# Fourteen products of constants on the TensorE between the router's products and the rank counts of a mixture-of-experts layer

## Chip, cores and metric

The kernel runs on one core of a Trainium2 chip, in one launch. The metric is device time in microseconds (us), the median over executions; the kernel before has 1560.44 us (median of 3 executions, 1560.36 to 1561.08).

## What is computed

One decoder layer in float32 on 256 tokens of width 2048, with 16 learned tokens in front. A combined input projection feeds three kinds of heads (HGRN2, mLSTM, Mamba-2), an output projection and a residual follow, then the part that matters here, a mixture of 32 experts with its router. Cut from the reference:

```
t = rmsnorm(h)                                    # 256 tokens x 2048 (and 16 that are dropped)
g_sel    = argmax(t @ w_group + b_group)          # one of 4 groups
e_logits = t @ w_router[g_sel] + b_router         # 8 experts in the group
top_v, top_i = top_k(e_logits, 2)                 # two experts for a token
rank of a token inside its expert = how many tokens before it chose the same expert
for every expert e, on the rows of its tokens:
    hidden = silu(xb @ w1[e]) * (xb @ w3[e]);  y = hidden @ w2[e]
out[token] += y * weight
```

## The kernel before

The program is written by hand, one instruction stream for each engine, ordered by semaphores; nothing is scheduled by a planner, so each queue runs in the order of the source.

**Up to the router.** The TensorE makes 52 input tiles of 272 columns (`tile`, `product`, line 1231) with the heads' products between them, then 16 output tiles of 256 columns (`mixed`, line 1274). After each output tile `by_rows` turns it into rows by two transposes (line 1471) and adds its part of the router's logits (line 1476, 36 columns). After the last `by_rows` the TensorE waits for semaphore `pairs`.

**Routing.** Meanwhile ScalarE sums squares (line 732) and VectorE runs `routing` (lines 292 to 332): logits, best group, two best experts, and `chosen`, a table of ones and zeros, tokens by experts. Line 332 signals `pairs`. The TensorE then counts ranks: five products with 32 columns each through `product` (line 1231 again, into bank 7), and signals `ranks`. VectorE makes the rank table (lines 335, 337) and the choice of rows for the first expert (line 1118).

**Experts.** An expert holds up to 32 token rows. For each one the TensorE does, in this order: `up` (line 1528: w1 in its first half, w3 in its second), `tokens` for the next expert (line 1511), `turn_hidden` (line 1536), `turn_tokens` (line 1518), `combine` of the expert before (line 1563: 8 products that use 32 of the 128 rows, each followed by an addition on VectorE, line 1145), `spread` (line 1543) and `down` (line 1552: w2). For expert 0 `tokens(0)` and `turn_tokens(0)` stand ahead of `up(0)`, with a copy by ScalarE after each (lines 744 and 748).

**Weights.** Each expert has three matrices of 4 MB (w1, w3, w2), so 96 transfers, all issued by SyncE's queue into four slots of SBUF. The first two are issued during the output projection (lines 416 and 418), the third and fourth after the last output tile and the last router product (lines 420 and 423). Every later one (lines 429, 433, 436) waits until the product that read its slot is done; the fifth waits for the first half of `up(0)`:

```
            sp.dma_start(eslot(3), matrix(1, 0)).then_inc(m_in[3], 16)
            used = (s["h1_ps"], s["h3_ps"], s["y_ps"])
            for m in range(4, 16):
                sp.wait_ge(used[(m - 4) % 3], (m - 4) // 3 + 1)
                sp.dma_start(eslot(m % 4), matrix(m // 3, m % 3)).then_inc(m_in[m % 4], 16)
```

**The end.** After the last transfer the TensorE still has the second half of `up(31)`, a `combine`, `down(31)` and a `combine`; ScalarE and VectorE then normalise and the result is stored. PSUM bank 1, `pb[1]`, is used by `spread` alone, first for expert 0. `ones` is a constant tile of 128 rows and 272 columns, filled at the start; T is 272, P 128.

Of the kernel before, what the change touches and what calls it, by code (L numbers as in the profile page):

```python
# [28 lines left out]
def hymba_moe_layer(nc, x, meta_tokens, hg_lb_logits, norm_mix_w, w_in, hg_norm_w, ml_b_i, ml_b_f,  # L29
# [11 lines left out]
    P = 128  # L41
# [3 lines left out]
    T = NM + SEQ  # L45
# [38 lines left out]
    FROM = [NM if t in range(Z0, Z0 + 8) or t in range(HQ, HQ + 4) or t in range(HG_, HG_ + 4)  # L84
            or t in range(MQ, MQ + 2) or t in range(MO, MO + 4) else 0 for t in range(NP_)]
    AT = {t0: sum(m for _, m in ORDER[:i]) for i, (t0, n) in enumerate(ORDER)}
    NIN, NOUT = NP_, KD

# [9 lines left out]
    with ctx:  # L98
        def sb(name, shape, dt=f32):
            return ctx.enter_context(nc.sbuf_tensor(name, shape, dt))  # L100
# [57 lines left out]
        ones = sb("ones", [P, T])  # L158
# [30 lines left out]
        pb = [ctx.enter_context(nc.psum_tensor(f"bank{i}", [P, 512], f32)) for i in range(8)]  # L189
# [350 lines left out]
        def _(act):  # L540
# [21 lines left out]
            for a, (_, n) in enumerate(TT):  # L562
                act.wait_ge(X_IN[a][0], 16 * X_IN[a][1])
                if a:
                    act.wait_ge(s["act_steps"], step.n)
                step.link(V.activation(junk[0:n, :], xin[0:n, a, :], ACT.Square, accum_out=ss3[0:n, a:a + 1]))
# [234 lines left out]
        def _(dve):  # L801
# [17 lines left out]
            for a, (_, n) in enumerate(TT):  # L819
                last = V.tensor_scalar(dg[0:n, a, 0:n], ident[0:n, 0:n], rs3[0:n, a:a + 1], None, ALU.mult)  # L820
# [403 lines left out]
        def _(pe):  # L1224
            V = nc.tensor
# [240 lines left out]
            def by_rows(k):  # L1466
                pe.wait_ge(s["in_ev"], 4 + NIN + k + 1)
                if k % 4 == 0 and k:
                    pe.wait_ge(s["t_ev"], NA * (k // 4))
                for a in range(NA):  # L1470
                    last = V.transpose(pb[5 + a][:, (k % 4) * P:(k % 4 + 1) * P],
                                       hT[:, k, NM + a * P:NM + (a + 1) * P], ident[:, :])
                    if k % 4 == 3:
                        last.then_inc(s["t_ps"], 1)
                for a in range(NA):
                    last = V.matmul(pb[(4, 7)[a]][:, 0:LG], hT[:, k, NM + a * P:NM + (a + 1) * P], wr[:, k, :],
                                    start=k == 0, stop=k == KD - 1)
                if k == KD - 1:
                    last.then_inc(s["lg_ready"], 1)
# [17 lines left out]
                by_rows(u - NIN - 1)  # L1497
            by_rows(NOUT - 1)

            pe.wait_ge(s["pairs"], 1)  # L1500
            for a in range(NA):
                product(pb[7][:, a * NE:(a + 1) * NE],
# [135 lines left out]
```

## Time and profile before

| | |
|---|---|
| median of 3 executions | 1560.44 us (1560.36 to 1561.08) |
| the profiled execution: its own time | 1565.83 us |
| the profiled execution: span of its instructions | 1564.1 us |
| TensorE busy | 1437.0 us (92%) |
| VectorE, ScalarE, GpSimd busy | 445.7, 310.0, 43.6 us |
| mean granted TensorE clock | 0.868 of full |
| read from HBM | 482.21 MB, 310 GB/s over the span |
| expert weights | 96 transfers of 4096 KB |

All durations of the trace are from the one profiled execution, whose time lies 5.39 us above the median. A granted clock of 1.00 is 2.4 GHz and one of 0.50 is 1.2 GHz; a number between them is a mean over a stretch. A float32 product stands in the trace as two matmul records, a transpose as one, so the five rank counts are ten records.

### The profile page before, as it was taken

The numbers are of one execution on the slowest core, as the hardware profiler recorded it, in microseconds if no ns is written. First come the engines' busy times: TensorE is split into PE (matmuls) and PEld (weight loads), VectorE is DVE, ScalarE is ACT, GpSimd is POOL, SyncE is SP. The second block draws the span as 40 slices with busy tenths as digits, with TensorE's granted clock in tenths as the row PEclk, the third lists the DMA queues.
The fourth block names the chain that finished last, engine by engine and source line by source line (L and its number), as shares of the span: only waits on it lengthen the run. The fifth ranks groups of instructions, "written<-read, shape, count | busy, mean of one in ns | idle before, by whom it ended". The sixth has DMA issues, their size and how long they took to land.

```text
span 1564.1 us, 18289 instructions
## 1 busy us (share of the span) xinstructions
PE 1437.0 (92%) x7667; PEld 786.7 (50%) x7667; DVE 445.7 (28%) x1033; ACT 310.0 (20%) x462; POOL 43.6 (3%) x77
## 2 busy tenths in 40 slices
PE   6999999999999997989988999889989998988986
PEld 3888888878888885323323323323323323323331
DVE  4312543341222002443312312212212313222213
ACT  2111423112123011212111112112112112112112
POOL 2000000000000011000000000000000000000002
PEclk9999999999999997888787688788788788788786
DMA  6444343445346645899999999999999999999992
GB/s 172 144 137 132 106 118 108 127 142 158 108 151 252 228 149 215 362 436 430 431 430 429 433 432 432 431 431 432 432 432 431 431 432 433 432 431 431 432 430 100
DMA packets 103512, 485.05 MB, mean 310 GB/s; under 512 B 19580, under 2 KB 89368, under 8 KB 90648
## 3 DMA queue, kind: packets, MB, share of 16 engines
q1 hardware_dynamic: 101424, 478.78, 75.9%
q0 software_dynamic: 1024, 3.37, 0.7%
q10 hardware_dynamic: 1016, 2.19, 0.4%
q8 instruction: 38, 0.62, 0.2%
q14 instruction: 10, 0.08, 0.0%
HBM read 482.21 MB, written 2.12 MB: 310 GB/s over the span
## 4 chain that ended last, share of the span: by engine, by line
PE 66%; DMA 30%; DVE 2%; ACT 1%; issue 0%; SPq 0%; ACTq 0%; DVEq 0%
DMA big<-in_moe_w_dram 30%; PE bank L1231 25%; PE bank L1563 9%; PE bank L1528 8%; PE bank L1274 7%; PE bank L1552 6%; PE bank L1511 2%; PE bank L1536 2%; DVE big L1145 2%; PE bank L1308 1%; PE bank L1287 1%; PE bank L1242 1%; PE bank L1259 1%; PE bank L1543 1%; DMA big<-in_x_dram 1%; PE bank L1352 1%
## 5 line engine op out<-in xcount | busy, mean ns | idle before, releaser
L1231 PE MATMUL bank<-big 128*128 128x272 f32 (+1 forms) x1664 | 380.1, 388 | 0.0
L1231 PEld LDWEIGHTS bank<-big 128*128 128x128 f32 x1664 | 313.6, 190 | 54.8 <-issue 0.4
L1563 PE MATMUL bank<-big 32*128 32x512 f32 x512 | 281.2, 935 | 32.8 <-DVE big L1145 31.8
L1528 PE MATMUL bank<-big 128*32 128x512 f32 x2048 | 239.7, 611 | 56.5 <-DMA big<-in_moe_w_dram 55.8
L1145 DVE TENSOR_TENSOR big<-big,bank 128x512 f32<-128x512 f32 x256 | 168.5, 685 | 165.1 <-PE bank L1563 163.9
L1563 PEld LDWEIGHTS bank<-big 32*128 32x128 f32 x512 | 94.6, 251 | 175.0 <-DVE big L1145 164.4
L1552 PE MATMUL bank<-big 128*32 128x512 f32 x1024 | 179.8, 866 | 0.1
L1528 PEld LDWEIGHTS bank<-big 128*32 128x32 f32 x2048 | 62.2, 112 | 228.0 <-issue 144.8
L1132 DVE COPY big<-bank 128x512 f32<-128x512 f32 x32 | 22.1, 692 | 415.0 <-PE bank L1528 415.0
L761 ACT ACTIVATE big<-bank 128x512 f32<-128x512 f32 x32 | 19.1, 597 | 481.6 <-PE bank L1552 481.6
L1274 PE MATMUL bank<-big 128*128 128x256 f32 x512 | 113.9, 381 | 0.0
L1274 PEld LDWEIGHTS bank<-big 128*128 128x128 f32 x512 | 96.3, 190 | 12.6
L1552 PEld LDWEIGHTS bank<-big 128*32 128x32 f32 x1024 | 39.8, 152 | 121.5 <-issue 121.2
L593 ACT ACTIVATE big<-bank 128x272 f32<-128x272 f32 (+1 forms) x52 | 20.4, 392 | 297.1 <-PE bank L1231 297.1
L1536 PEld LDWEIGHTS bank<-selq,big 128*128 128x128 f32 x512 | 59.6, 191 | 26.8 <-issue 26.8
L1511 PE MATMUL bank<-big 128*32 128x512 f32 x512 | 62.5, 607 | 1.2 <-DVE big L1118 1.2
L1536 PE MATMUL bank<-selq,big 128*128 128x32 f32 x512 | 63.1, 277 | 0.0
L744 ACT ACTIVATE big<-bank 128x512 f32<-128x512 f32 x32 | 19.1, 597 | 214.9 <-PE bank L1511 214.9
L752 ACT ACT_TABLE_LOAD x31 | 39.8, 1283 | 0.6
L757 ACT ACT_TABLE_LOAD x31 | 39.8, 1283 | 0.6
L1113 DVE TENSOR_TENSOR big<-big,bank 128x256 f32<-128x256 f32 x16 | 6.7, 421 | 110.9 <-PE bank L1274 110.9
L1511 PEld LDWEIGHTS bank<-big 128*32 128x32 f32 x512 | 16.6, 111 | 39.8 <-issue 39.8
(261 smaller groups left out, 762.0 us busy)
## 6 DMA issues: line engine op xcount, KB each, us to landing
big<-in_moe_w_dram SPq DMA_DIRECT2D x96, 4096.0 KB, 30.4
big<-in_w_in_dram SPq DMA_DIRECT2D x26, 2048.0 KB, 8.3
big<-in_w_out_dram SPq DMA_DIRECT2D x8, 2048.0 KB, 8.4
big<-gate_rows POOLq DMA_DIRECT2D x8, 272.0 KB, 3.8
out_dram<-big SPq DMA_DIRECT2D x4, 512.0 KB, 3.9
big<-gate_rows POOLq DMA_DIRECT2D x2, 544.0 KB, 5.8
big<-in_x_dram SPq DMA_DIRECT2D x1, 1024.0 KB, 8.3
big<-in_norm_ffn_w_dram ACTq DMA_DIRECT2D x1, 1024.0 KB, 4.3
```

What stands on the lines that cost most here:

```text
L593: V.activation(proj[:, TILES[u], FROM[TILES[u]]:T], pb[u % 4][:, FROM[TILES[u]]:T], func).then_inc(s["in_ev"], 1)
L752: V.activation(hs1.rearrange("t (k p) -> t k p", p=P), pb[2][:, :].rearrange("t (p k) -> t k p", k=KF), ACT.Copy).then_inc(s["h1_ev"], 1)
L757: V.activation(ssb, pb[4][:, 0:KF * CAP], ACT.Silu).then_inc(s["silu_ev"], 1)
L1132: V.tensor_copy(hs3.rearrange("t (k p) -> t k p", p=P), pb[3][:, :].rearrange("t (p k) -> t k p", k=KF)).then_inc(s["h3_ev"], 1)
L1145: V.tensor_tensor(h2[:, a, d * 512:(d + 1) * 512], h2[:, a, d * 512:(d + 1) * 512], pb[6 + j % 2][:, :], ALU.add).then_inc(s["y_acc"], 1)
L1231: last = V.matmul(outs, a, b, start=start and j == 0, stop=stop and j == n - 1)
L1274: last = V.matmul(pb[u % 4][:, 0:SEQ], wchunk(c % 2)[:, k, u % 2 * P:(u % 2 + 1) * P], proj[:, MIXED[k], NM:T], start=k == 0, stop=k == 7)
L1511: last = V.matmul(pb[0][CAP * g:CAP * (g + 1), :], oh[:, a, :], u2[:, a, g * 512:(g + 1) * 512], start=a == 0, stop=a == NA - 1)
L1528: last = V.matmul(pb[2 + r][CAP * g:CAP * (g + 1), :], xsT[:, j, g, :], w[:, 4 * g + j, :], start=j == 0, stop=j == 3)
L1536: last = V.matmul(pb[4][:, (r * KF + k) * CAP:(r * KF + k + 1) * CAP], hs[:, k * P:(k + 1) * P], selq[:, :], start=True, stop=True)
L1552: last = V.matmul(pb[5][CAP * g:CAP * (g + 1), :], hTb[:, k * CAP:(k + 1) * CAP], w[:, k, g * 512:(g + 1) * 512], start=k == 0, stop=k == ...
L1563: V.matmul(pb[6 + j % 2][:, :], wT[CAP * g:CAP * (g + 1), a * P:(a + 1) * P], ysb[CAP * g:CAP * (g + 1), :], start=True, stop=True).then_i ...
```

## The change

Fourteen products are put into the TensorE's stream, after the last `by_rows` and ahead of the wait for `pairs`. Their operands are the constant tile `ones` (128 rows by 128 columns as weights, 272 columns streamed), and they write columns 0 to 271 of bank 1. They wait for nothing and signal nothing, and nothing reads what they write; `spread(0)` overwrites it later.

```
             by_rows(NOUT - 1)
 
+            for _ in range(14):
+                V.matmul(pb[1][:, 0:T], ones[:, 0:P], ones[:, :], start=True, stop=True)
+
             pe.wait_ge(s["pairs"], 1)
             for a in range(NA):
```

On the TensorE, between the last router products (line 1476) and the rank counts (line 1231, with `before` or `ones` as weights), the program now reads:

```order
 L1471 MATMUL bank<-ident,big 128x128 x2
 L1476 MATMUL bank<-wr,big 128x36 x2
+L1501 MATMUL bank<-ones 128x272 x14
 L1231 MATMUL bank<-big,before 128x32
 L1231 MATMUL bank<-big,ones 128x32
```

Nothing else moved, on this engine or on the others; only the line numbers behind the insertion are three higher.

## Rows read from the trace of the kernel before

**Rows 1.** The page, the span in 40 slices: granted clock, DMA busy share, GB/s.
```profile
PEclk9999999999999997888787688788788788788786
DMA  6444343445346645899999999999999999999992
GB/s 172 144 137 132 106 118 108 127 142 158 108 151 252 228 149 215 362 436 430 431 430 429 433 432 432 431 431 432 432 432 431 431 432 433 432 431 431 432 430 100
```
**Rows 2.** Waits of the TensorE: who waited for whom, total us, times, longest us.
```profile
PE bank L1528 <- DMA big<-in_moe_w_dram: 55.8, 29, 3.8
...
PE bank L1231 <- DVE big L332: 8.4, 1, 8.4
```
**Rows 3.** SyncE's queue, issues: start us, us, line, what, count.
```profile
605.00 0.34 SPq L420 DMA_DIRECT2D big<-in_moe_w_dram  x1
606.38 0.34 SPq L423 DMA_DIRECT2D big<-in_moe_w_dram  x1
630.56 3.76 SPq L429 DMA_DIRECT2D big<-in_moe_w_dram  x2
```
**Rows 4.** Busy time by stretch: us, PE, PEld, DVE, ACT, POOL (records), clock, DMA, GB/s.
```profile
605.90:608.95 3.05, 0.39 (x5) 0.28 (x3) 1.37 (x5) 2.80 (x8) 0.75 (x1) 1.00 0.97 344
608.95:614.67 5.72, 0.00 (x0) 0.00 (x0) 5.26 (x24) 1.18 (x2) 3.02 (x2) 0.50 1.06 458
...
624.35:629.44 5.09, 5.09 (x24) 1.18 (x28) 0.00 (x0) 1.24 (x1) 0.00 (x0) 0.50 0.25 106
629.44:630.56 1.12, 1.12 (x16) 0.36 (x12) 0.00 (x0) 0.00 (x0) 0.00 (x0) 1.00 0.00 0
627.00:631.50 4.50, 4.50 (x36) 1.10 (x32) 0.00 (x0) 0.60 (x1) 0.00 (x0) 0.73 0.00 0
...
631.50:1531.50 900.00, 813.24 (x4685) 285.12 (x4678) 253.72 (x548) 161.20 (x217) 0.00 (x0) 0.80 1.00 430
```
**Rows 5.** Timeline of the TensorE, 604 to 640: start us, us, what, idle before.
```profile
605.76 0.53 PE L1476 MATMUL bank<-wr,big 128*128 128x36 f32 x4
614.68 0.64 PE L1231 MATMUL bank<-big,before 128*128 128x32 f32 x2 [8.38 <-DVE big L332]
...
618.20 3.64 PE L1511 MATMUL bank<-big 128*32 128x512 f32 x16 [1.18 <-DVE big L1118]
622.55 1.11 PE L1518 MATMUL bank<-ident,big 128*128 128x128 f32 x4 [0.71 <-ACT big L744]
624.35 9.57 PE L1528 MATMUL bank<-big 128*32 128x512 f32 x64 [0.69 <-ACT big L748]
633.75 1.89 PE L1511 MATMUL bank<-big 128*32 128x512 f32 x16
635.57 1.97 PE L1536 MATMUL bank<-selq,big 128*128 128x32 f32 x16
637.37 0.63 PE L1518 MATMUL bank<-ident,big 128*128 128x128 f32 x4
```
**Rows 6.** Chain that ended last: start us, us, what.
```profile
199.12 7.33 PE bank L1231 x32
...
614.68 2.36 PE bank L1231 x10
...
641.92 3.48 PE bank L1528 x32
```
**Rows 7.** Busy time by stretch in experts and tail, columns as in rows 4.
```profile
652.80:656.70 3.90, 2.95 (x10) 0.98 (x9) 2.40 (x5) 0.60 (x1) 0.00 (x0) 1.00 1.17 494
656.70:662.60 5.90, 5.83 (x10) 2.07 (x10) 2.95 (x5) 0.00 (x0) 0.00 (x0) 0.50 0.97 417
...
808.30:810.30 2.00, 2.00 (x13) 0.55 (x16) 1.00 (x4) 0.00 (x0) 0.00 (x0) 0.50 0.93 393
810.40:815.00 4.60, 4.60 (x48) 1.32 (x44) 0.00 (x0) 1.88 (x2) 0.00 (x0) 1.00 1.04 449
849.60:854.70 5.10, 5.10 (x24) 1.18 (x28) 0.00 (x0) 0.00 (x0) 0.00 (x0) 0.50 1.00 430
...
1527.14:1536.20 9.06, 8.50 (x14) 3.25 (x14) 4.38 (x8) 0.00 (x0) 0.00 (x0) 0.50 0.33 129
1536.25:1540.79 4.54, 4.54 (x25) 1.19 (x28) 0.54 (x2) 0.00 (x0) 0.00 (x0) 0.50 0.00 0
```

## The prediction

> **What bounds the kernel now.** I read the page's slices first. From slice 17 to slice 39 the DMA engines are full at some 431 GB/s, while the clock wanders between 0.7 and 0.8 [rows 1]. The stretch from 631.5 to 1531.5 us has a DMA share of 1.00 at 430 GB/s [rows 4], and in the list of waits the TensorE waits for expert weights 29 times, 55.8 us in all [rows 2]. So the expert stage lasts as long as its transfers last. TensorE time inside it is worth nothing; what counts is when the row of transfers starts to run without a break, and the short end behind it.
>
> I then looked for that start. SyncE issues weights 3 and 4 at 605.00 and 606.38, and the next one only at 630.56 [rows 3], when the first half of `up(0)` has freed a slot. From 627.0 to 631.5 no byte moves [rows 4]. That hole of **4.5 us** lies on the path: the issue of 630.56 is about 1.0 us ahead of the first byte, so every microsecond by which the first half of `up(0)` ends sooner brings the end forward by one, until the hole is closed at 4.5.
>
> What sets the end of that half is a chain without slack from the last router product at 605.76. The TensorE waits 8.38 us for VectorE's routing, then come rank counts, a VectorE piece, `tokens(0)`, a copy, `turn_tokens(0)`, a copy, `up(0)` [rows 5]. The granted clock is 1.00 up to 608.95, 0.50 from there to 629.44 and 1.00 again afterwards [rows 4]. It fell after 2.65 us in which the TensorE did nothing (606.30 to 608.95), so the whole chain ran at 1.2 GHz, and it came back 5.09 us after `up(0)` had begun.
>
> **The change part by part.** *The products themselves.* 16 products of 272 columns at full clock take 7.33 us, two records each [rows 6], thus 0.458 us for one and 6.41 us for 14. They begin when the router's products end, near 606.30, and end near 612.7. VectorE lets the rank counts go at 614.68, so 2.0 us are left: cost nothing, covered by the 8.38 us wait, as long as the clock stays full. If that cover went, because they ran at 1.2 GHz throughout, they would take 12.8 us and end at 619.1, 4.4 us late; the doubling follows from `tokens`, 3.64 us at 1.2 GHz and 1.89 at 2.4 [rows 5]. Bank 1 has no other use before `spread(0)` at about 637.8, VectorE and ScalarE keep their work, and no DMA is touched: nothing.
>
> *The clock at the rank counts.* With the TensorE busy until 612.7 and idle 2.0 us, less than the 2.65 us after which it fell, I take the counts at full clock. They took 2.36 us for 10 records at half clock [rows 6]; 16 records of 32 columns at full clock took 1.97 [rows 5], so ten take 1.2. Gain **1.2 us**, bounds 0 (the clock has already fallen) and 1.3.
>
> *The clock from there to `up(0)`.* This is the open term. Behind the counts the TensorE waits another 1.1 us for VectorE, and around the copies twice 0.7. Between 612.7 and 617.1 it does little but small products, and the trace shows that idle time alone is not what lets the clock fall: from 652.8 to 656.7 it was busy for 2.95 of 3.90 us with 32-row products, and fell at 656.7 all the same [rows 7]. So I expect the clock to fall once more after the counts, before or in `tokens(0)`. What is then gained depends on when it comes back. Before, `up(0)` spent 5.09 us at half clock. In the expert loop dense products had run between 2.1 us (808.25 to 810.34) and 5.1 us (849.6 to 854.7) when it came back [rows 7]; 5.09 is at the slow end of these. With the middle, 3.6, the stretch at half clock is 1.5 us shorter, and each microsecond of it costs half a microsecond against full clock: gain **0.7 us**. Lower bound: it comes back later in the work than before. The half of `up(0)` would then run at half clock to its end, 6.8 us (twice the 3.48 us of [rows 6] less its end) where it took 6.1, a loss of 0.7. Upper bound: the clock never falls. Then the chain from 614.68 is 1.2 (counts), 1.1 (VectorE), 1.9 (`tokens`), 0.7, 0.6 (`turn_tokens`), 0.7 and 3.5 (half of `up`), which ends at 624.4, 6 us sooner than 630.5, of which the hole lets 4.5 count.
>
> **Sum:** 0 - 1.2 - 0.7 = -1.9 us. From the profiled execution's 1565.83 that gives 1563.9; its 5.39 us over the median are carried over unchanged, so 1560.44 - 1.9 = **1558.5 us**. I do not know that the other executions have the same hole. If the clock comes back earlier in them already, their hole is smaller, and so is what can be won. A measurement of this kernel can tell about 0.2% from no change, 3.1 us, so my forecast is "within 0.2%".
>
> **The rivals.** *Full clock throughout* (0.17). The fill products leave no idle stretch as long as 2.65 us before `up(0)`; if only idle time counts, the clock holds, the hole closes and the gain is 4.5: 1555.9 us. The fall at 656.7 in the middle of work speaks against it. The Trainium skill (TensorE: Matmul & The Clock Gate, Why this matters for your kernels) advises just this, to keep idle gaps between bursts of products short; by that rule taken alone this rival would be the forecast.
>
> *Nothing won* (0.20). The clock falls in the thin stretch and comes back one step later in the work than before, so that what the counts gain, the products behind them give back: 1560.4 us, and at most 0.7 more. For it speaks that `tokens(0)`, 3.64 us of dense work at half clock, did not bring the clock back before [rows 4, 5], so its return is a matter of where it falls.
>
> *Constants do not hold the clock* (0.08, slower). If products of ones do not count as work, the clock falls at 608.95 as before. 2.65 of 6.41 us of work are then done and 3.76 take 7.5: the fill ends at 616.5, and the rank counts start 1.8 us late, with all behind them: 1562.2 us. It decides from the point where more than 2.0 us of the fill run at half clock; with all of it there, 4.4 us, 1564.9. For it speaks only that no row shows constant operands over a long stretch.
>
> *The end lands differently* (0.08). After the transfers the TensorE is the bound. It ran 9.06 us at half clock from 1527.14, and 4.54 of `down(31)` [rows 7]. A row of transfers that ends earlier shifts where these falls and returns come: plus or minus 2 us on any of the cases, from the 5.1 and 2.1 us above (half of 3.0 is 1.5) and a little for the additions that wait. This is in the range.
>
> **How the numbers follow.** Forecast 0.47, full clock 0.17, nothing won 0.20, constants 0.08, end 0.08. Faster by over 0.2% needs 3.1 us: the full-clock case mostly, and the forecast where the clock returns at once or the end helps: 0.24. Slower by over 0.2%: the slower rival only near its full price, or with a bad end: 0.05. Within: 0.71. The range goes from the full-clock case, 1555.7, to the nothing-won case with 1 us of bad end, 1561.4; it leaves out the slower rival.
>
> **What would show it.** Right: records of the 14 products, 28 of them, from 606.3 to 612.7 at clock 1.00; the counts in 1.2 us; a fall of the clock near 615 to 618 instead of 608.95; the fifth weight transfer issued near 628.6 instead of 630.56 and a hole of 2.6 us; the same 431 GB/s to the end. The issue near 625 and no hole mean full clock throughout. Wrong: a fall of the clock inside the fill, the counts beginning after 614.7, a hole as long as before, or a time that moves without the hole moving, which would put the cause in the end behind the transfers.

## The result and the profile after

With the 14 products the kernel takes 1563.34 us (median of 20 executions, 1559.80 to 1567.64), beside 1560.70 us before (median of 20, 1559.68 to 1563.80). The ratio is 1.0015, 95% interval 1.0009 to 1.0021: slower by 2.6 us. I had forecast 1558.5 and a range up to 1561.4.

The times lie in groups. Of the 20 before, 15 are between 1559.7 and 1561.4 and 5 between 1562.7 and 1563.8. With the 14 products 4 are below 1561.1 and 16 from 1562.8 up. A profile shows one of the timed executions (the one below has 1564.98 us, which is among the 20), so its own time says which group it belongs to. The profile that I predicted from, 1565.83 us, was an execution 2 us longer than any of those 20. In this comparison and those below the kernel before ran 121 times in all: 3 of these executions took 1565.6 to 1565.9 us, 30 took 1562.3 to 1563.8, and the rest less. That matters below.

The TensorE of the kernel with 14 products (timeline: start us, us, what, idle before) does what was expected up to the rank counts:

```profile
605.84 6.66 PE L1501 MATMUL bank<-ones 128*128 128x272 f32 x28
614.51 0.41 PE L1231 MATMUL bank<-big,before 128*128 128x32 f32 x2 [2.01 <-DVE big L332]
...
617.38 3.64 PE L1514 MATMUL bank<-big 128*32 128x512 f32 x16 [1.18 <-DVE big L1118]
621.73 1.11 PE L1521 MATMUL bank<-ident,big 128*128 128x128 f32 x4 [0.71 <-ACT big L744]
623.53 9.72 PE L1531 MATMUL bank<-big 128*32 128x512 f32 x64 [0.69 <-ACT big L748]
```

28 records end 2.01 us ahead of the counts, where the wait was 8.38 us [rows 5]. The clock and the transfers by stretch (us, PE, PEld, DVE, ACT, POOL, clock, DMA, GB/s):

```profile
605.84:612.50 6.66, 6.66 (x30) 5.22 (x29) 4.99 (x16) 3.54 (x8) 3.88 (x2) 1.00 0.97 396
615.33:628.98 13.65, 11.07 (x53) 3.48 (x56) 3.58 (x17) 2.48 (x3) 0.00 (x0) 0.50 0.72 310
...
627.00:630.50 3.50, 3.50 (x28) 0.88 (x24) 0.00 (x0) 0.60 (x1) 0.00 (x0) 0.73 0.00 0
...
631.00:1531.00 900.00, 815.94 (x4686) 284.29 (x4678) 254.26 (x548) 161.21 (x217) 0.00 (x0) 0.80 1.00 430
```

The clock held through the fill, fell within the rank counts and came back at 629.0, where [rows 4] had 608.95 and 629.44. Nothing moves from 627.0 to 630.5, and behind that the transfers run at the same 430 GB/s. The fifth transfer is issued at 629.89:

```profile
629.89 3.76 SPq L429 DMA_DIRECT2D big<-in_moe_w_dram  x2
```

So against [rows 3] this profile is 0.7 us better, 0.3 of it since its router products end sooner, and its time is 0.9 us shorter than 1565.83. Profile against profile the change helps a little; by the timed executions it costs 2.6. One of the two profiles had to be untypical, and the experiments had to find which.

### The profile page after: what moved, and what is told of

It is laid out like the page before. It is cut to its first block, busy times and chain, and to the rows that moved or that the text cites. A ratio compares the mean times of both kernels' runs of the same rounds, so it can differ in the third digit from the quotient of the medians.

```text
span 1563.1 us, 18345 instructions
## 1 busy us (share of the span) xinstructions
PE 1445.4 (92%) x7695; PEld 790.4 (51%) x7695; DVE 445.6 (29%) x1033; ACT 310.0 (20%) x462; POOL 44.2 (3%) x77
## 4 chain that ended last, share of the span: by engine, by line
PE 66%; DMA 30%; DVE 2%; ACT 1%; issue 0%; SPq 0%; ACTq 0%; DVEq 0%
DMA big<-in_moe_w_dram 29%; PE bank L1231 25%; PE bank L1566 9%; PE bank L1531 8%; PE bank L1274 7%; PE bank L1555 6%; PE bank L1514 2%; PE bank L1539 2%; DVE big L1145 2%; PE bank L1308 1%; PE bank L1287 1%; PE bank L1242 1%; PE bank L1259 1%; PE bank L1546 1%; DMA big<-in_x_dram 1%; PE bank L1352 1%
## 5 line engine op out<-in xcount | busy, mean ns | idle before, releaser
L1531 PE MATMUL bank<-big 128*32 128x512 f32 x2048 | 243.1, 619 | 53.9 <-DMA big<-in_moe_w_dram 53.2
L1555 PE MATMUL bank<-big 128*32 128x512 f32 x1024 | 181.6, 874 | 0.1
L1514 PE MATMUL bank<-big 128*32 128x512 f32 x512 | 62.5, 607 | 1.2 <-DVE big L1118 1.2
```

The costliest lines, as they stand in the source:

```text
L1514: last = V.matmul(pb[0][CAP * g:CAP * (g + 1), :], oh[:, a, :], u2[:, a, g * 512:(g + 1) * 512], start=a == 0, stop=a == NA - 1)
L1531: last = V.matmul(pb[2 + r][CAP * g:CAP * (g + 1), :], xsT[:, j, g, :], w[:, 4 * g + j, :], start=j == 0, stop=j == 3)
L1555: last = V.matmul(pb[5][CAP * g:CAP * (g + 1), :], hTb[:, k * CAP:(k + 1) * CAP], w[:, k, g * 512:(g + 1) * 512], start=k == 0, stop=k == ...
```

## The experiments

Three theories. **A**: what counts is where the clock falls against `tokens(0)`. In most executions of before it falls early, `tokens(0)` brings it back, and `up(0)` runs at full clock, with a small hole (a hole is the stretch in which no byte moves ahead of the fifth weight transfer); with the 14 products the fall comes later and `tokens(0)` no longer does this. **B**: the holes are alike, and the loss lies behind the last transfer. **C**: the products themselves delay something.

### Other fills

`e1_hold` fills every wait up to `up(0)`; `e1_fill18` and `e1_fill7` change the 14; `e1_late` has only the later fills of `e1_hold`. `fill(n)` makes n of the same products.

```
e1_hold:    by_rows(NOUT - 1)       + fill(18)
            rank counts             + fill(2)
            tokens(0)               + fill(1)
            turn_tokens(0)          + fill(1)
e1_late:    as e1_hold without fill(18)
e1_fill18, e1_fill7:   range(14) -> range(18), range(7)
```

> Fill products at every wait between the router's products and up(0): 18 ahead of the rank counts, 2 behind them, 1 behind tokens(0), 1 behind turn_tokens(0). Theory A (the loss is the place where the clock falls: in most timed executions of before, tokens(0) alone brings the clock back ahead of up(0), and with the fall postponed to 615.4 us it no longer does): the clock holds at 1.00 to up(0), the fifth weight transfer is issued near 625, no hole in the transfers, some 1.2 us faster than before: 1559.2 us. Theory B (the loss lies behind the last transfer, where the clock's falls and returns come elsewhere): the hole closes, the time is like that with the 14 products, 1563. Theory C (the products themselves cost, by delaying something): slower than the 14 products, 1564 or more.

> 18 products in place of 14, so that they end at about 614.1 us, 0.4 us before the rank counts. Theory A: the stretch with little work is 1.8 us shorter, the clock holds or comes back in more of the executions: between 1559 and 1561 us. Theory B: like 14 products, 1563. Theory C: slower than 14, 1564.

> 7 products in place of 14, ending near 609.1 us. Theory A: the clock falls 0 to 3.4 us later than before but still well ahead of tokens(0), which brings it back as before: time as before, 1560.7 us, and its values grouped as before's are. Theory B: no clear forecast, between 1560.7 and 1563. Theory C: half the loss, 1562.

> No products ahead of the rank counts; only the 2 behind them, 1 behind tokens(0), 1 behind turn_tokens(0). The clock has fallen by then as in before. Theory A: the fillers run at half clock, 1.8 us for the two behind the counts against a wait of 1.1, so tokens(0) starts some 0.7 us later, and 0.2 us are lost behind each of the other waits; but the work is without a break, so that the clock is back at the latest early in up(0): 1560 to 1561.5. Theory B: like before or up to 2 us off. Theory C: about 1562.

Medians of 11 executions each, beside 1561.04 us for before (33 executions): `e1_hold` 1560.26 (ratio 0.9991, 0.9982 to 1.0000), `e1_fill18` 1561.09 (1.0003, 0.9994 to 1.0012), `e1_fill7` 1561.43 (1.0004, 0.9995 to 1.0013), `e1_late` 1561.63 (1.0002, 0.9993 to 1.0012). More fill than 14 is not slower than 14, and `e1_hold` has the 14 and eight more: theory C falls. `e1_late`, in which the clock had fallen as in the kernel before, was no faster than it either. In `e1_hold` the clock never falls before `up(0)`:

```profile
614.80:628.00 13.20, 12.74 (x102) 5.37 (x106) 3.49 (x17) 3.07 (x4) 0.00 (x0) 1.00 1.00 417
```

The transfers have no break there, and the fifth is issued at 624.94. Yet its profiled execution, the slowest of the 11, took 1563.26 us, since its end was long; B has a part too. `e1_fill7`, in which the clock fell 6.0 us behind the last router record, shows theory A's return in `tokens(0)`: `turn_tokens(0)` took 0.66 us and `up(0)` 7.07.

The profile of `e1_fill18` (1559.75 us) is as telling. It fills the first wait alone, up to 0.18 us ahead of the counts, and leaves the three gaps behind them, and the clock did not fall before `up(0)` or in it; there was no hole:

```profile
606.35 8.50 PE L1501 MATMUL bank<-ones 128*128 128x272 f32 x36
...
617.50 1.92 PE L1514 MATMUL bank<-big 128*32 128x512 f32 x16 [1.18 <-DVE big L1118]
...
621.48 7.07 PE L1531 MATMUL bank<-big 128*32 128x512 f32 x64 [0.69 <-ACT big L748]
```

Its 11 executions lie in two groups, 6 up to 1561.1 us and 5 from 1562.7 up, so that may not hold in all of them.

### The same program 1.8 us later

Four more of the products go ahead of the last output tile, where the TensorE is the bound. They delay everything behind, and nothing else, in the kernel before and in the one with 14.

```
             for u in range(NIN + 2, NIN + NOUT):
+                if u == NIN + NOUT - 1:
+                    for _ in range(4):
+                        V.matmul(pb[1][:, 0:T], ones[:, 0:P], ones[:, :], start=True, stop=True)
                 out_tile(u)
```

> The kernel before with 4 of the same products (1.83 us at full clock) put ahead of the last output tile, where the TensorE is the bound: everything behind starts 1.8 us later and nothing else changes, unless the place in time of the clock's falls and returns against the program matters. Theory A (the chip's falls and returns come at times that the program meets by its own timing, and what tokens(0) does about the clock hangs on that): the clock falls some 3.5 us behind the last router product, tokens(0) no longer brings it back, the hole in the transfers is 3 to 4.7 us; time 1560.9 + 1.8 + 1.5 to 3, so 1564 to 1565.5 us. Theory B (the loss comes from the end behind the transfers): hole in the profile as before, about 1.3 to 4.5. Theory D (timing does not matter): 1562.7 us.

> The same shift by 4 products in the kernel with the 14. Theory A: the clock falls while or just after the rank counts run, early enough for tokens(0) to bring it back: hole 0 to 1 us, 1560.5 to 1562.5 us, so it is FASTER than the shifted kernel before, by 2 to 4 us, where without the shift it was 2.6 us slower. Theories B and D: 2.6 us slower than the shifted kernel before.

The shifted kernel before takes 1567.17 us (1565.19 to 1567.44, 7 executions, ratio to before 1.0032, 1.0020 to 1.0043), the shifted one with 14 products 1563.70 (1561.38 to 1565.99, 11 executions, 1.0013, 1.0004 to 1.0022), beside 1561.10. **The sign turns**: here the 14 products make it 3.5 us faster. The two intervals just touch, but six of the 7 executions of the first lie above all 11 of the second. The medians lie 1.7 and 1.2 us above the ranges that I had expected, but no theory in which the products have a fixed price gives this. The profiles: in the shifted kernel before the clock fell 3.7 us behind the last router record, where I had expected 3.5, and was at half up to 631.8, `up(0)` included, and the fifth transfer left at 632.26, 25.2 us behind the start of the last router products (607.07). With the 14 it was back at 627.9 and the transfer left at 629.86, 22.9 us behind them (606.92). The hole was 4.9 us long in the first and 1.6 in the second, the end 44.2 and 43.2 us. The way there was not the one that I had expected: `tokens(0)` ran at half clock from its start at 618.45 and did not bring the clock back; it came back 3.3 us into `up(0)`.

```profile
611.30:631.80 20.50, 13.24 (x62) 5.10 (x66) 7.80 (x41) 2.69 (x4) 1.97 (x2) 0.51 0.77 333
```

```profile
617.75:627.90 10.15, 8.06 (x37) 2.19 (x40) 3.18 (x16) 2.48 (x3) 0.00 (x0) 0.51 0.85 368
627.95:640.00 12.05, 12.00 (x114) 4.98 (x110) 3.82 (x17) 3.35 (x5) 0.00 (x0) 1.00 0.79 320
```

### Fills in the end

I tried to quiet the end, to see the hole alone and to gain time. Here the fills are written out; `e2_tail` and `e2_hold_tail` also have one product of 272 columns ahead of the last `combine`.

```
 combine, last two:  each product followed by
+    V.matmul(pb[0][:, 0:192], ones[:, 0:P], ones[:, 0:192], start=True, stop=True)   (e2_tail, e2_hold_tail)
+    if j % 2: V.matmul(pb[0][:, 0:T], ones[:, 0:P], ones[:, 0:T], ...)               (e3_pairs and the two below)
```

> Only the end is changed: one product of constants of 192 columns (0.32 us) behind each product of the last two combines, and one of 272 ahead of the last. All theories: clock at 1.00 from the last up to the end; combine 10.3 to 8 us, down(31) 5.9 to 3.6, the last combine partly bound by GpSimd's 9.85 us of multiplications: 4 to 5 us less than before, 1556.5. Theory B adds that the scatter of the times shrinks to less than half; theory A that a scatter of 3 us from the hole is left.

> Both: clock held to up(0), and in the end. Hole 0 and a short end: 1554.5 to 1555.5 us, some 5.5 us (0.35%) faster than before, with a scatter below 1.5 us if A and B together explain the scatter.

A plain miss: 1582.21 us (4 executions, ratio 1.0134, 1.0119 to 1.0150), and 1579.37 with the clock held to `up(0)` (1.0112, 1.0097 to 1.0128). The first row below is a `combine` in `e4_before_a`, an execution of the kernel before, the others are `e2_tail`:

```profile
1521.01 1.13 PE L1563 MATMUL bank<-big 32*128 32x512 f32 x4
```

```profile
1521.48 1.12 PE L1567 MATMUL bank<-big 32*128 32x512 f32 x2
1522.53 0.59 PE L1237 MATMUL bank<-ones 128*128 128x192 f32 x2
...
1526.94 2.07 PE L1567 MATMUL bank<-big 32*128 32x512 f32 x2
1528.94 1.01 PE L1237 MATMUL bank<-ones 128*128 128x192 f32 x2
```

Four records, two products, took 1.13 us in the kernel before; here two records, one product, take 1.12. The two products use different 32 rows; by these times they run together, and with a product of 128 rows between them they do not. Sixteen products then cost more than the clock could give, and it fell all the same (2.07 us).

> The end again, with the product of constants (272 columns, 0.45 us) only behind every second product of the last two combines, where at full clock the TensorE waits 0.84 us for VectorE, so that two products of 32 rows still run at the same time. All theories: if the clock holds, combine 7.6 instead of 10.3 us, down(31) 3.6 instead of 5.9, the last combine bound by GpSimd: 4 us faster than before, 1557; if it falls in spite of it, each product at half clock adds 0.4 us: 1561.

> The 14 products with the same end as e3_pairs, so that the end is as alike as it can be. Theory A (the loss of the 14 is the hole): 1.5 to 2.6 us slower than e3_pairs. Theory B (the loss is the end): less than 0.5 us from e3_pairs.

> The clock held to up(0) as in e1_hold, and the end of e3_pairs. If the end works: no hole and a short end, 1554.5 to 1556 us, 0.35% faster than before and the fastest of all; if it does not, like e1_hold, 1560.

With the fill only behind every second product: `e3_pairs` 1562.48 us (1556.40 to 1568.44, ratio 0.9998, 0.9982 to 1.0014), `e3_14_pairs` 1563.37 (1556.56 to 1565.66, 1.0001, 0.9987 to 1.0014), `e3_hold_pairs` 1560.26 (1559.51 to 1562.50, 0.9989, 0.9981 to 0.9998), 12 executions each, before 1561.36. Where the clock holds in the end, as in the profile of `e3_pairs`, `down(31)` takes 3.64 us (5.87 in the first profile of the kernel before, 5.57 in `e4_before_a`) and the end behind the last wait for weights is 40.5 us instead of 43.2 to 44.2; where it falls, as in that of `e3_14_pairs`, nothing is won. The scatter of 12 us made the comparison of 14 with 0 products useless: inconclusive for A against B. Their profiles up to the last wait are two more samples, since only the end differs from the kernels under test; they are used below.

```profile
1530.86 3.64 PE L1556 MATMUL bank<-big 128*32 128x512 f32 x32
```

### More profiles of the two kernels themselves

> The kernel with the 14 products once more, for a second profile and for its times beside the others on this chip. Theory A: in the profile the hole follows from where the clock falls: a fall 9.5 us behind the last router product goes with no return in tokens(0) and a hole of 3.6 us; a fall nearer to 10.3 us goes with a return 3 us sooner and a hole of 1 to 2. Median 2 to 3 us above before.

> The kernel before, unchanged, for its profile. Theory A: the clock falls 1 to 2.7 us behind the last router product's start and is back by the end of tokens(0), some 16 us behind it; hole 1 to 1.7 us; time near 1560.5. If the fall is later than 2.9 us, the return is in up(0), the hole 4.5 and the time near 1563.5. Theory B: hole 4.5 us at a time of 1560.5, with a shorter end.

> As e4_before_a: theory A wants the time to follow the hole, 1560.5 with a hole of 1 to 1.7 us and 1563.5 with one of 4.5.

> As e4_before_a: theory A wants the time to follow the hole, 1560.5 with a hole of 1 to 1.7 us and 1563.5 with one of 4.5.

> The kernel with the 14 products, for its profile. Theory A: the clock falls 9.4 to 10 us behind the last router product's start, returns in up(0), hole 3 to 4 us, time 1563 to 1565; or, with a fall before 9.3 or behind 10 us, a hole of 0 to 1.7 us and a time near 1561. Theory B: time 1563 or more with a hole no larger than that of the kernel before at its usual time.

> The kernel with the 14 products, a further profile. Theory A: return of the clock in up(0), hole 2.5 to 4 us, end behind the last wait for weights 44.2 us, time 1562.8 to 1565; where the hole is below 1.7 us, a time near 1561.

> The clock held to up(0), again. Theory A: no hole; time 1 to 1.5 us below before where the end is like before's 43.2 us, and the same as before or 0.5 us above where it is 45.8 us, so median 0 to 1.5 us below before.

`e3_14_again` had a median of 1562.06 us (12 executions) beside 1561.36, ratio 1.0003 (0.9994 to 1.0011), less than the first comparison; `e5_hold_b` 1560.90 (11 executions) beside 1560.69, ratio 0.9998 (0.9989 to 1.0007). All profiles side by side, counted from the start of the last router record; "end" is from the start of the second half of `up(31)`, the last that waits for weights, to the end of the span:

| profiled execution | clock falls | returns | hole | to the last wait | end | its time, us |
|---|---|---|---|---|---|---|
| before, the predicted one | 2.9 | 23.4 | 4.5 | 913.9 | 44.2 | 1565.83 |
| e4_before_a | 5.0 | 15.2 | 1.0 | 910.7 | 43.2 | 1560.58 |
| e4_before_b | 2.1 | 15.8 | 1.7 | 910.8 | 43.2 | 1560.73 |
| e4_before_c | 5.0 | 15.2 | 0.9 | 910.6 | 43.2 | 1560.69 |
| after | 9.5 | 23.2 | 3.6 | 913.2 | 44.2 | 1564.98 |
| e3_14_again | 11.8 | 22.0 | 2.4 | 912.3 | 44.2 | 1562.96 |
| e4_14_a | 12.0 | 22.2 | 2.7 | 912.3 | 44.2 | 1562.86 |
| e5_14_b | 9.1 | 15.9 | 1.0 | 910.8 | 43.2 | 1561.18 |
| e1_hold | no | | 0 | 909.6 | 45.8 | 1563.26 |
| e5_hold_b | no | | 0 | 911.0 | 43.2 | 1560.89 |

This is the answer. All three new profiles of the kernel before have the clock back by the end of `tokens(0)` and a hole of 0.9 to 1.7 us; three of the four with 14 products have it back only in `up(0)`, and a hole of 2.4 to 3.6. The one exception, `e5_14_b`, is also the one with a time like before's. The profiles in which only the end was changed agree: without the 14 products `e2_tail` and `e3_pairs` have the clock back 15.7 and 16.3 us behind the record and holes of 1.5 and 1.6, with them `e3_14_pairs` has it back at 23.3, with a hole of 3.2. That makes a late return, in `up(0)`, in one of six profiles without the products and in four of five with them. The quarter of before's executions that took 1562.3 to 1563.8 us is in no profile. Here is `e4_before_a`, the TensorE and the stretches around the return, then the issue:

```profile
617.10 3.39 PE L1511 MATMUL bank<-big 128*32 128x512 f32 x16 [1.18 <-DVE big L1118]
621.21 0.66 PE L1518 MATMUL bank<-ident,big 128*128 128x128 f32 x4 [0.71 <-ACT big L744]
```

```profile
610.40:617.62 7.22, 2.86 (x14) 2.44 (x18) 4.30 (x25) 0.21 (x1) 0.47 (x1) 0.50 0.99 427
617.62:620.64 3.02, 2.87 (x16) 0.46 (x8) 1.67 (x9) 0.08 (x1) 0.00 (x0) 0.59 1.08 467
620.64:623.08 2.44, 1.19 (x12) 0.65 (x16) 0.43 (x2) 1.67 (x3) 0.00 (x0) 1.00 1.00 423
```

```profile
626.25 18.61 SPq L429 DMA_DIRECT2D big<-in_moe_w_dram  x5
```

`up(0)` begins at 622.55 and its first half frees the slot 3.7 us later. And `e4_14_a`, in which `tokens(0)` begins at 615.87, still at full clock, first by stretch, then its issue:

```profile
615.98:616.70 0.72, 0.72 (x8) 0.20 (x9) 0.58 (x5) 0.00 (x0) 0.00 (x0) 0.93 1.69 728
616.70:621.40 4.70, 3.32 (x20) 1.04 (x16) 1.86 (x8) 1.28 (x3) 0.00 (x0) 0.50 1.02 439
621.40:626.90 5.50, 5.50 (x28) 1.33 (x32) 0.00 (x0) 1.20 (x1) 0.00 (x0) 0.51 0.47 203
```

```profile
627.76 11.75 SPq L429 DMA_DIRECT2D big<-in_moe_w_dram  x3
```

The clock fell inside `tokens(0)`, the dense work by whose end it is back in the kernel before, and `up(0)` ran at half clock for nearly the whole of its first half, which took 6.4 us (621.35 to 627.76).

What decides whether `tokens(0)` brings the clock back is not shown. That the fall comes too near to it is not enough: in `after` it fell at 9.5 us, all of `tokens(0)` ran behind it, and no return came; in `e5_14_b` it fell at 9.1, just as much of `tokens(0)` ran behind it, and the clock was back right after it:

```profile
617.35 3.64 PE L1514 MATMUL bank<-big 128*32 128x512 f32 x16 [1.18 <-DVE big L1118]
621.70 0.66 PE L1521 MATMUL bank<-ident,big 128*128 128x128 f32 x4 [0.71 <-ACT big L744]
```

In the kernel before, falls at 2.1 and 5.0 us behind the last router record had the early return and the fall at 2.9 had not. So the places that I had expected failed: a fall later than 2.9 us was to mean a hole of 4.5 (`e4_before_a` and `e4_before_c`, 5.0, had 1.0 and 0.9), and a fall behind 10 us a small hole (`e4_14_a`, 12.0, had 2.7, and `e3_14_again`, 11.8, had 2.4). A difference of 0.5 us in the place of the fall goes with a return 7 us later here, and one of 0.3 us does so between `e3_pairs` (2.6) and the first profile (2.9); the 14 products changed which case is the usual one, and why they did is open.

Taken without the hole, the time from the last router record to the last wait is 909.6 to 909.9 us in seven of the ten rows, and 909.0, 909.4 and 911.0 in `e4_before_b`, the predicted execution and `e5_hold_b`: the transfers pass the hole on about one for one. `e5_hold_b` is 1.4 us longer than `e1_hold` there; why, I have not settled. In the other experiments the same sum lies between 908.4 (`e2_hold_tail`) and 910.4 us (`e1_fill7`, `e2_after_shift4`), so one for one holds within about 1 us.

The end is the second part. It took 43.2 us behind a hole of 0.9 to 1.7 us, and 44.2 behind one of 2.4 or more; of the executions without a hole `e5_hold_b` and `e1_fill18` had 43.2 and `e1_hold` 45.8. Why a long end goes with a large hole is not shown. It differs by how much of it meets full clock. In `e4_before_a`, whose last wait ends at 1515.54, nearly the first half of `combine(30)` (from 1521.01) does; in `e4_14_a` (wait 1516.89, `combine(30)` from 1522.36) the clock falls 2.3 us into it:

```profile
1516.10:1525.10 9.00, 7.97 (x57) 3.64 (x50) 3.23 (x6) 0.28 (x1) 0.00 (x0) 0.97 0.89 377
1525.20:1535.40 10.20, 10.02 (x34) 3.07 (x37) 3.15 (x6) 0.00 (x0) 0.00 (x0) 0.53 0.07 27
```

```profile
1517.00:1524.60 7.60, 6.76 (x53) 3.25 (x53) 1.99 (x4) 0.28 (x1) 0.00 (x0) 1.00 0.94 400
1524.70:1538.30 13.60, 13.57 (x42) 3.97 (x44) 4.66 (x8) 0.00 (x0) 0.00 (x0) 0.50 0.16 67
```

## Why the prediction was wrong

*What bounds the kernel: right.* The transfers bound the expert stage, the hole is on the path and passes on about one for one, and what it waits for is the first half of `up(0)`.

*The products cost nothing by themselves: right.* 6.66 us, over 2.01 us ahead of the counts, at full clock; `e1_hold` has more of them and is not slower.

*"The clock at the rank counts", gain 1.2 us: right in kind, a little too large.* From the start of the counts to `tokens(0)` took 3.52 us (614.68 to 618.20), then 2.87 in the profile after, where the clock fell within the counts, and 2.49 in `e4_14_a`: 0.65 to 1.0 us.

*"The clock from there to up(0)", gain 0.7, lower bound a loss of 0.7: this step failed, by its base.* The second fall came where I had said. But I priced the return against the 5.09 us at half clock of [rows 4] and took this as what executions of before do. It was the rare case. In the three further profiles the first half of `up(0)` took 3.7 us, all at full clock; with the 14 products it took 6.2 to 6.4 in three of four. `tokens(0)` and `turn_tokens(0)` with their copies took 5.5 us on average without them and 5.8 in those three. The term is not -0.7 but **+2.9 us**; less the 0.9 that those three gained on average at the counts that is +2.0 on the chain. The holes agree: 3.6, 2.4 and 2.7 have a mean of 2.9, and 1.0, 1.7 and 0.9 one of 1.2, so 1.7 more; the last wait is at 912.6 against 910.7, 1.9 more. The lower bound should have been the loss of a return in `tokens(0)`, a row of 3.64 us of dense work that I had in front of me.

*"Its 5.39 us over the median are carried over unchanged": wrong.* I took them to belong to the profile. The three profiles at 1560.6 to 1560.7 show 3.2 us of them in the hole and to the last wait and 1.0 in the end; the rest is the start, since the last router product comes 1.0 to 1.1 us earlier in them. A profile 5.4 us over the median of its kernel is a sign that it shows an unusual execution, and I wrote the right warning ("if the clock comes back earlier in them already, their hole is smaller") but gave it no chance of its own on the slower side.

*The rivals.* "Nothing won" had the mechanism, the return one step later in the work, with at most 0.7 us on top instead of 2.6. "Full clock throughout" did not occur in the four profiles with 14 products. In the profile after, until the fall at 615.3, the TensorE had no idle stretch longer than 2.01 us, and the clock fell; so the advice of the Trainium skill (TensorE: Matmul & The Clock Gate, Why this matters for your kernels) to keep the gaps between bursts short did not suffice here. The clock did hold in `e1_hold`, with the gaps filled as well, and in `e1_fill18`, where 18 products leave 0.18 us ahead of the counts and the later gaps of 1.18, 0.71 and 0.69 us stay. "Constants do not hold the clock" is refuted: it stood at 1.00 over 6.66 us of them. "The end lands differently" occurred, 1.0 us, and in the same executions as the large hole; I had taken it as independent.

*The range.* Its lower end is 1555.7, where the rival it is taken from gives 1555.9; nothing hangs on it. The end behind the transfers stood at 0 in the sum.

*The sum after the fact:* 1.7 to 1.9 us to the last wait and 1.0 in the end give 2.7 to 2.9, beside 2.64 between the medians. That rests on three usual profiles of each kernel, chosen by their return; with all four of each the mean hole differs by 0.4 us only, for there the rare 4.5 us of the first profile counts as one in four. So the sum shows what a usual execution of each loses, and agrees with the medians less closely than its digits say. The size is not a constant of the change: one further comparison gave 1.0003, and the shift by 1.8 us turned the sign. A version that reliably beats the kernel before was not found: `e1_hold` gave 0.9991 (0.9982 to 1.0000), then 0.9998 (0.9989 to 1.0007), and `e3_hold_pairs` 0.9989 (0.9981 to 0.9998), 0.1% at most.

## What to carry to other kernels

A fill in front of thin work may only postpone the fall of the clock, and the return can then come later too, in the piece that is on the path; here that turned a gain of 0.9 us at the counts into a loss. Judge such a fill by where the clock returns in several executions, and not by how long it holds. A longer fill (`e1_fill18`) and fills in every gap (`e1_hold`) kept the clock up in the executions that were profiled, and neither made the kernel clearly faster. Before pricing an edit from a profile, compare the profile's own time with the group that most executions lie in: where it is longer by more than their scatter, ask which of its stretches is the unusual one. And price a clock term from the state in which most executions meet it, with a bound for each dense piece that could lose its return.

## What the runs showed of the hardware

The same program meets the falls and returns of the clock at other places from one execution to the next: in the kernel before 2.1 to 5.0 us behind the last router record, with the 14 products 9.1 to 12.0. Between the first profile of the kernel before and `e4_before_a` that goes with 4.2 of 5.2 us, in the hole and the end, and four products that take 1.8 us by my estimate moved the median by 6.1 (1561.10 to 1567.17). Two products of 32 rows in different rows of the array ran in 1.13 us together and in 1.12 us each with a full-width product between them. A busy TensorE is no sign of a full clock: in `e1_fill18` it was at half from 1524.0 to 1534.2 with 9.92 of 10.20 us busy, 5.3 us of them in `combine`.
